# Router logits from the raw sums instead of the normed rows, with the first two experts' ranks computed apart

## The chip, the cores and the metric

The kernel runs on one core of a Trainium2 chip. The metric is the device time of one execution in microseconds (us), measured over several executions. The median of three runs of the kernel before is 3284.68 us (3284.26 to 3285.56).

## The reference, cut to what matters

The program is a stack of layers on 512 tokens of width 1024: two layers of a mixer, a cross attention and a dense feed-forward net (`first_block`), then one layer of attention, retention and a mixture of experts (`second_block`). The change touches what lies between the mixer's output sum and the experts:

```
h = h + mix                                   # the raw sum, x_tok
hn = h * rsqrt(mean(h*h) + 1e-6) * norm_moe_w # rms norm, row factor and column weights
group_logits  = hn @ w_group  + b_group       # 8 columns
expert_logits = hn @ w_expert + b_expert      # 64 columns
...
best group by softmax, its two best experts per token, gates from their softmax
every expert: (silu(hn_e @ w1) * (hn_e @ w3)) @ w2 on the tokens that chose it
h = h + sum of the two experts' rows times their gates
out = rms_norm(h, norm_final_w)
```

Since the row factor is one number per token and the norm weights are one number per column, `hn @ w` equals the row factor times `h @ (norm_moe_w * w)`.

## The kernel before, in words

Everything is fp32. Five engines run programs written out by hand, one method for each stage and engine (`merge_pe`, `router_dve` and so on), joined by counting semaphores; `at(mark)` is the semaphore value at which a step is done. PSUM banks are taken from and given back to one list (`Banks`), so a bank that is taken waits for whoever drained it last. NT = 4 tiles of 128 tokens; KD = 8 blocks of 128 columns.

**Mixer out.** `project_out_pe` multiplies by `w_out` in two halves of 512 columns. For the second half the tiles go in the order (0, 1), (2), (3), each over two weight pieces, twelve matmuls to a tile and piece. After tile 2 it calls `turned(0)`, which transposes the normed rows of tiles 0 and 1; inside tile 3, between its two pieces, it calls `turned(1)`, which does nothing. VectorE adds each half to the raw sum `x_tok` (`add_dve`), and after each tile's second half runs `normed(i)`: `rms_dve` makes the argument of the root, GpSimd takes the power (`root_pool`), VectorE writes the normed row to `hn_low` with its columns regrouped. ScalarE squares and sums the raw row first (`square_act`).

**Router.** `router_pe` transposes the normed rows of tiles 2 and 3 (`rows_to_T_pe_f32`), ScalarE copies them out of PSUM to `xT` (`hn_turned_act`), and 32 matmuls of 72 columns (64 records in the trace, since each fp32 matmul is recorded twice) make the logits. `router_dve` adds the bias and runs a chain of 20 small instructions, each of which waits for the one before, up to `both`, a 0/1 table of each token's two experts. Then `rank` (4 matmuls with a triangle and with ones: how many earlier tokens chose the same expert), `count` (4 matmuls of 64 columns), `local` (VectorE: the rank where the expert was chosen), and for each pair of experts `chosen`, a one-hot table with which TensorE gathers the tokens' rows (`gather_pe`, 16 matmuls for a pair). The gather reads the normed rows split in two, `hn_high` (ScalarE, rounded) and `hn_low` (VectorE, the rest, `hn_split_dve`).

**Experts.** 64 experts, each with three matrices of 2 MB. SyncE loads them in one fixed order into slots; a slot is free when a mark is reached. `experts_pe` declares eight slots: two of 1 MB (`att`, `outs`) used once, and six of 2 MB in this order: `mT` (free when the mixer's last tile is summed), `01`, `20`, `12` (free with the last weight pieces of the mixer), `norms` (free when tile 3's normed row is written, `("moe_norm", "rms", 3)`), `xT` (free when the logits are done). From then on a slot comes free when its expert's matmuls are done. For an expert TensorE runs `upper_pe` (w1 and w3, 16 matmuls, 32 records) and `lower_pe` (w2).

**Loads.** ScalarE's queue issues the router's small tables in `router_act`: `tri`, `router_w` (72 columns by 1024 rows; partition p holds rows 8p to 8p+7, one run of 2304 B for each partition), `router_b`, `down8`, `iota64`.

Of the kernel before, what the change touches and what calls it, by code (L numbers as in the profile page):

```python
# [12 lines left out]
ALU = mybir.AluOpType  # L13
# [51 lines left out]
PC_ALL = PC_GATE + 2 * KD  # L65
# [126 lines left out]
class Net:  # L192
# [2233 lines left out]
    def merge_dve(self, e):  # L2426
# [32 lines left out]
    def router_pe(self, e):  # L2459
        e.begin("router")  # L2460
        banks, at = self.banks, self.at
        W = GROUPS + EXPERTS
        bank = banks.take(e, "router")
        e.wait_ge(*at("router_tables", "iota"))
        for i in range(NT):
            if i % 2 == 0:
                self.rows_to_T_pe_f32(e, 2 + i // 2)
            for b in (0, 4):
                e.wait_ge(*at("hnT", i, b))
            for k in range(KD):  # L2470
                ins = e.matmul(bank[:, i * W:(i + 1) * W], self.xT[:, k, i * P:(i + 1) * P], self.router_w[:, k, :],
                               start=(k == 0), stop=(k == KD - 1))
            ins.then_inc(*(e.tick("pe", "router") if i == NT - 1 else e.tick()))
        banks.give(("router",), "logits")
        bank = banks.take(e, "rank")
        e.wait_ge(*at("both"))
        e.wait_ge(*at("ones"))
        both = self.both.rearrange("p i e -> p (i e)")
# [6 lines left out]
        bank = banks.take(e, "count")  # L2485
# [4 lines left out]
        banks.give(("count",), "counted")  # L2490

    def rows_to_T_pe_f32(self, e, i):
        for b in (0, 4):
            bank = self.banks.take(e, "hnT", i, b)
            e.wait_ge(*self.at("moe_norm", "rms", i))
            self.transposes(e, bank, [self.hn_low[:, i, (b + j) * P:(b + j + 1) * P] for j in range(4)]).then_inc(
                *e.tick("pe", "hnT", i, b))
            self.banks.give(("hnT", i, b), "hnT", i, b)

    def router_act(self, e):  # L2500
# [3 lines left out]
        for name, dst, src in (("tri", self.tri, a["c_tri"]),  # L2504
                               ("w", self.router_w, a["router_w"].rearrange("(p t) n -> p t n", p=P)),
# [4 lines left out]
        for i in range(NT):  # L2510
            self.square_act(e, i, self.hn_high[:, i, :], "moe_norm", ("merge_out", "added", 1, i))
            if i:
                self.hn_turned_act(e, i - 1)
                self.hn_high_act(e, i - 1)
        self.hn_turned_act(e, NT - 1)
        self.hn_high_act(e, NT - 1)

    def hn_high_act(self, e, i):

        self.high_of(e, self.hn_high[:, i, :], self.hn_low[:, i, :]).then_inc(*e.tick("hn_high", i))  # L2520

    def hn_split_dve(self, e, i):

        e.wait_ge(*self.at("pe", "hnT", i, 4))
# [36 lines left out]
    def router_dve(self, e):  # L2561
# [32 lines left out]

        e.wait_ge(*at("pe", "rank"))
        e.scalar_tensor_tensor(out=self.local.rearrange("p i e -> p (i e)"), in0=self.both.rearrange("p i e -> p (i e)"),
                               scalar=FAR, in1=self.bank("rank")[:, 0:NT * EXPERTS], op0=ALU.mult,
                               op1=ALU.subtract).then_inc(*e.tick("local"))

# [80 lines left out]
    def gather_pe(self, e, q):  # L2680

        ch = self.chosen[q % 2]
        for half in range(2):
# [4 lines left out]
            for i in range(NT):  # L2688
# [52 lines left out]
    def experts_pe(self, e):  # L2741
# [16 lines left out]
        self.rows_T_pe(e, 0)  # L2758
        self.upper_pe(e, 0)
# [103 lines left out]
    def experts_dve(self, e):  # L2863
        e.begin("experts")
        for n in range(EXPERTS + 1):
            if n < EXPERTS and n % 2 == 0:
# [3 lines left out]
                for i in range(NT):  # L2870
                    e.tensor_tensor(self.rounded(self.chosen[n // 2 % 2][:, i, :, :]),
                                    self.from_far.unsqueeze(1).broadcast_to([P, 2, CAP]),
                                    self.local[:, i, n:n + 2].unsqueeze(2).broadcast_to([P, 2, CAP]),
                                    ALU.is_equal).then_inc(*(e.tick("chosen", n // 2) if i == NT - 1 else e.tick()))
# [293 lines left out]
def columns(inputs):  # L3168
# [17 lines left out]
    out[:, PC_GATE:PC_GATE + 2 * KD] = tile(np.asarray(inputs["b_branch_gate_2"])[0])  # L3186
    return out
# [37 lines left out]
```

## Time and profile before

| | |
|---|---|
| median of 3 runs | 3284.68 us |
| the profiled execution, its own time | 3284.82 us |
| its span, first to last instruction | 3283.0 us |
| mean granted TensorE clock | 0.976 of full speed |
| PE (TensorE matmul) busy | 3094.9 us, 94% |
| DVE (VectorE) busy | 1389.0 us, 42% |
| ACT (ScalarE) busy | 887.1 us, 27% |
| POOL (GpSimd) busy | 134.4 us, 4% |
| DMA | 627.49 MB, 191 GB/s over the span |
| DMA in the last quarter | 426 to 430 GB/s in each fortieth of the span |

The profile is of one execution. Times in its rows are us from the start of the span; a duration named mean or min/median/max is in ns. "PEld" is the loading of weights, which overlaps matmuls. "SPq" and "ACTq" are the instructions with which SyncE and ScalarE start DMAs. A matmul's end is modelled, so neighbouring matmuls overlap in the rows, and their pace is read from start to start. The share of busy time says little here, since the stages differ: the first 2240 us are held by TensorE, the last 900 by the loads.

### The profile page before, as it was taken

To read this page: it belongs to the slowest core of one execution; us is meant where nothing else is said; L and a number is where in the kernel's file an instruction comes from. 1 tells how busy PE (TensorE), PEld (TensorE's weight loads), DVE (VectorE), ACT (ScalarE), POOL (GpSimd) and SP (SyncE) were. 2 spreads that over 40 slices of the span, in tenths; PEclk is the share of its full clock that TensorE was granted. 3 is DMA by queue.
4 is the path that set the end of the run, shared out by engine and by line. 5 is a ranking of instruction groups with operands and counts; after the bars stand their busy time and mean duration, and the time that the engine had idled before them with its cause. 6 is when DMAs were issued, how large, how long until landed. Compare 5 with 4: busy or idle time off the path is not lost.

```text
span 3283.0 us, 34804 instructions
## 1 busy us (share of the span) xinstructions
PE 3094.9 (94%) x14748; PEld 2159.3 (66%) x14748; DVE 1389.0 (42%) x2291; ACT 887.1 (27%) x1408; POOL 134.4 (4%) x118
## 2 busy tenths in 40 slices
PE   9999999999999999999999899998999889999995
PEld 7678688887677778888888787886434334434332
DVE  5675543335586553334777576434211111111112
ACT  3452322222343322222344432332111111111111
POOL 0000000001000000000211010000000000000001
PEclk9999999999999999999999999999999999999998
DMA  5122122333222222322322430235999999999997
GB/s 178 52 77 97 57 93 97 100 108 118 65 64 86 69 80 87 109 97 96 110 68 68 119 102 33 81 112 229 401 429 429 430 429 429 428 426 429 428 429 304
DMA packets 197794, 627.49 MB, mean 191 GB/s; under 512 B 11712, under 2 KB 129216, under 8 KB 172672
## 3 DMA queue, kind: packets, MB, share of 16 engines
q1 hardware_dynamic: 176288, 581.46, 45.5%
q10 hardware_dynamic: 19152, 35.61, 3.0%
q0 software_dynamic: 2192, 8.13, 0.9%
q8 instruction: 118, 1.93, 0.2%
q14 instruction: 44, 0.36, 0.0%
HBM read 600.26 MB, written 22.81 MB: 190 GB/s over the span
## 4 chain that ended last, share of the span: by engine, by line
PE 75%; DVE 10%; DMA 8%; ACT 3%; issue 2%; POOL 2%; ACTq 0%; SPq 0%; DVEq 0%
PE bank L121 72%; PE bank L124 3%; DMA pieces<-in_moe_w 3%; DVE gate_acc L139 2%; DMA highs<-in_moe_w 2%; DMA piece_high<-in_moe_w 2%; DVE x_tok L139 1%; POOL root L136 1%; DVE piece_rounded L136 1%; DVE stat L154 1%; ACT piece_high_rounded L127 1%; DVE probs L142 1%; DVE aprobs L142 1%; ACT probs L127 1%; DVE qs L136 1%
## 5 line engine op out<-in xcount | busy, mean ns | idle before, releaser
L136 DVE TENSOR_TENSOR piece_rounded<-piece,piece_high_rounded 128x2048 fp32r<-128x2048 f32 (+2 forms) x160 | 346.7, 2171 | 527.6 <-ACT piece_high_rounded L127 527.5
L121 PE MATMUL bank<-xT_rounded,piece_high_rounded 128*128 128x512 f32 (+1 forms) x1424 | 541.4, 380 | 12.1 <-DVE xT_low_rounded L136 7.2
L121 PE MATMUL bank<-xT_low_rounded,piece_high_rounded 128*128 128x512 f32 (+1 forms) x1424 | 538.7, 378 | 0.0
L121 PE MATMUL bank<-xT_rounded,piece_rounded 128*128 128x512 f32 (+1 forms) x1424 | 538.4, 378 | 0.0
L136 DVE TENSOR_TENSOR gate_and_hidden<-gate_and_hidden,bank 64x512 f32<-64x512 f32 x64 | 69.3, 1082 | 801.8 <-ACT gate_and_hidden L127 801.8
L127 ACT ACTIVATE piece_high_rounded<-piece 128x2048 fp32r<-128x2048 f32 (+2 forms) x160 | 288.1, 1804 | 254.6 <-DMA piece<-in_ffn_w_down 91.5
L121 PEld LDWEIGHTS bank<-xT_rounded,piece_high_rounded 128*128 128x128 f32 x1424 | 269.1, 189 | 64.2 <-DVE xT_low_rounded L136 8.2
L121 PEld LDWEIGHTS bank<-xT_rounded,piece_rounded 128*128 128x128 f32 x1424 | 269.1, 189 | 49.4
L121 PEld LDWEIGHTS bank<-xT_low_rounded,piece_high_rounded 128*128 128x128 f32 x1424 | 269.1, 189 | 48.1
L121 PE MATMUL bank<-mT_pair,xeT 128*64 128x512 f32 x352 | 178.8, 667 | 22.8 <-issue 22.8
L121 PE MATMUL bank<-xT,xeT 128*64 128x512 f32 x336 | 172.4, 673 | 23.0 <-issue 22.6
L121 PE MATMUL bank<-memory_norms,xeT 128*64 128x512 f32 x320 | 167.1, 683 | 22.2 <-issue 22.2
L127 ACT ACTIVATE gate_and_hidden<-bank 64x512 f32<-64x512 f32 x64 | 37.8, 591 | 479.0 <-PE bank L121 479.0
L139 DVE SCALAR_TENSOR_TENSOR gate_acc<-hT,cols,gate_acc 128x512 f32<-128x512 f32 x240 | 163.2, 743 | 0.0
L121 PE MATMUL bank<-highs,xeT 128*64 128x512 f32 x352 | 155.6, 595 | 2.0 <-DMA pieces<-in_moe_w 2.0
L121 PE MATMUL bank<-piece_high,xeT 128*64 128x512 f32 x352 | 155.6, 595 | 1.9 <-DMA highs<-in_moe_w 1.9
L121 PE MATMUL bank<-pieces,xeT 128*64 128x512 f32 x320 | 141.5, 595 | 1.4 <-DMA piece_high<-in_moe_w 1.4
L121 PE MATMUL bank<-piece_high_rounded,hidT_rounded 128*128 128x512 f32 x352 | 137.3, 390 | 0.0
L121 PE MATMUL bank<-piece_high_rounded,hidT_low_rounded 128*128 128x512 f32 x352 | 137.1, 389 | 0.0
L121 PE MATMUL bank<-piece_rounded,hidT_rounded 128*128 128x512 f32 x352 | 137.1, 389 | 0.0
L121 PE MATMUL bank<-piece_high_rounded,xT_rounded 128*128 128x512 f32 (+1 forms) x320 | 120.9, 378 | 5.3 <-DVE xT_low_rounded L136 2.7
L136 POOL TENSOR_TENSOR root<-root,power 128x1 f32<-128x1 f32 (+2 forms) x60 | 61.0, 1016 | 1444.5 <-DVE root L133 1444.4
(344 smaller groups left out, 4903.1 us busy)
## 6 DMA issues: line engine op xcount, KB each, us to landing
mT_pair<-in_moe_w SPq DMA_DIRECT2D x32, 2048.0 KB, 16.5
pieces<-in_moe_w SPq DMA_DIRECT2D x32, 2048.0 KB, 16.5
piece_high<-in_moe_w SPq DMA_DIRECT2D x32, 2048.0 KB, 16.4
highs<-in_moe_w SPq DMA_DIRECT2D x32, 2048.0 KB, 16.7
xT<-in_moe_w SPq DMA_DIRECT2D x32, 2048.0 KB, 16.7
memory_norms<-in_moe_w SPq DMA_DIRECT2D x31, 2048.0 KB, 16.7
piece<-in_ffn_w_in SPq DMA_DIRECT2D x40, 1024.0 KB, 5.0
piece<-in_w_in SPq DMA_DIRECT2D x20, 1024.0 KB, 4.8
```

Of the source, the lines that this page charges most:

```text
L121: return self.engine.matmul(*a, **k) if self.engine is not None else Nothing()
L124: return self.engine.transpose(*a, **k) if self.engine is not None else Nothing()
L127: return self.engine.activation(*a, **k) if self.engine is not None else Nothing()
L136: return self.engine.tensor_tensor(*a, **k) if self.engine is not None else Nothing()
L139: return self.engine.scalar_tensor_tensor(*a, **k) if self.engine is not None else Nothing()
L142: return self.engine.tensor_tensor_reduce(*a, **k) if self.engine is not None else Nothing()
L154: return self.engine.bn_stats(*a, **k) if self.engine is not None else Nothing()
```

## The change

Four edits. (1) The transposes read `x_tok`, the raw sum, instead of the normed row; tile 2's transposes and the logits of tiles 0 and 1 stand in `turned(1)`, between the two pieces of tile 3. (2) The column weights go into `router_w` by one VectorE multiplication (its load uses the plain row order now, 1024 runs of 288 B, and the norm weights come with the table `cols`); the row factor goes in where the bias is added, tile by tile. (3) Tile 3's normed row is written after `both`; its square on ScalarE comes after the copies of its transposes. (4) The ranks of experts 0 and 1 are made first from 8, 6, 4 and 2 columns, then the whole rank; the counts come after the first gather and its transposes. The slots `xT` and `norms` change places.

```diff
         def turned(i):
-            if i:
+            if i == 0:
+                for j in (0, 1):
+                    self.rows_to_T_pe_f32(e, j)
                 return
+            self.banks.take(e, "router", 0)
             for j in (0, 1):
-                self.rows_to_T_pe_f32(e, j)
+                self.logits_pe(e, j)
+            self.rows_to_T_pe_f32(e, 2)
...
         def normed(i):
-            self.rms_dve(e, i, self.hn_low[:, i, :], self.gain[:, :], "moe_norm", ("moe_norm", "gain"), KD)
+            if i == 0:
+                e.wait_ge(*at("router_tables", "iota"))
+                e.tensor_tensor(self.router_w, self.router_w,
+                                self.cols[:, PC_NORM:PC_NORM + KD].unsqueeze(2).broadcast_to([P, KD, GROUPS + EXPERTS]),
+                                ALU.mult).then_inc(*e.tick("router_w"))
+            if i < NT - 1:
+                self.rms_dve(e, i, self.hn_low[:, i, :], self.gain[:, :], "moe_norm", ("moe_norm", "gain"), KD)
...
+        bank = banks.take(e, "first_rank")
         e.wait_ge(*at("both"))
         e.wait_ge(*at("ones"))
+        e.matmul(bank[:, 0:2 * NT], self.tri, self.both[:, :, 0:2], start=True, stop=False).then_inc(*e.tick())
+        for n in range(1, NT):
+            ins = e.matmul(bank[:, 2 * n:2 * NT], self.ones, self.both[:, 0:NT - n, 0:2], start=False, stop=(n == NT - 1))
...
     def rows_to_T_pe_f32(self, e, i):
...
-            e.wait_ge(*self.at("moe_norm", "rms", i))
-            self.transposes(e, bank, [self.hn_low[:, i, (b + j) * P:(b + j + 1) * P] for j in range(4)]).then_inc(
+            e.wait_ge(*self.at("merge_out", "added", 1, i))
+            self.transposes(e, bank, [self.x_tok[:, i, (b + j) * P:(b + j + 1) * P] for j in range(4)]).then_inc(
...
-                               ("w", self.router_w, a["router_w"].rearrange("(p t) n -> p t n", p=P)),
+                               ("w", self.router_w, a["router_w"].rearrange("(t p) n -> p t n", p=P)),
...
-        for i in range(1, NT):
+        for i in range(1, NT - 1):
             self.hn_split_dve(e, i)
-        e.wait_ge(*at("pe", "router"))
-        e.tensor_tensor(logits, self.bank("router")[:, 0:NT * W].rearrange("p (i w) -> p i w", i=NT),
-                        self.row(self.router_b, W), ALU.add).then_inc(*e.tick("logits"))
+        for i in range(NT):
+            if i == NT - 1:
+                self.rms_arg_dve(e, i, "moe_norm")
+            e.wait_ge(*at("pe", "router", max(i, 2)))
+            e.wait_ge(*at("root", "moe_norm", i))
+            e.scalar_tensor_tensor(out=logits[:, i, :], in0=self.bank("router", i // 3)[:, i * W:(i + 1) * W],
+                                   scalar=self.root[:, i, 0:1], in1=self.router_b, op0=ALU.mult,
+                                   op1=ALU.add).then_inc(*e.tick("logits", i))
...
-
+        self.rms_row_dve(e, NT - 1, self.hn_low[:, NT - 1, :], self.gain[:, :], "moe_norm", ("moe_norm", "gain"), KD)
+        first = self.local[:, :, 0:2]
+        e.wait_ge(*at("pe", "first_rank"))
...
+        self.chosen_dve(e, 0)
+        self.hn_split_dve(e, NT - 1)
...
+        self.add_slot("xT", self.xT[:, :, :].rearrange("p k s -> p (k s)"), ("pe", "router", NT - 1))
         self.add_slot("norms", memory, ("moe_norm", "rms", NT - 1), ("pe", "m_branch", "retention", KD - 1))
-        self.add_slot("xT", self.xT[:, :, :].rearrange("p k s -> p (k s)"), ("pe", "router"))
...
         self.rows_T_pe(e, 0)
+        self.count_pe(e)
```

The order of the instructions on TensorE from tile 2's transposes to the last logits, before (`hn_low` is the normed row, `mT` the mixer's merged input, `xT` the transposed rows):

```order
L124 MATMUL bank<-ident,hn_low 128x128 [waits merge_vector_done,side_loads]
L124 MATMUL bank<-ident,hn_low 128x128 x7
L121 MATMUL bank<-router_w,xT 128x72 [waits router_scalar_done]
L121 MATMUL bank<-router_w,xT 128x72 x7
...
L124 MATMUL bank<-ident,hn_low 128x128 [waits merge_vector_done]
L124 MATMUL bank<-ident,hn_low 128x128 x7
```

and in the change, from the end of tile 3's first piece over its second to tile 3's transposes:

```order
L122 MATMUL bank<-router_w,xT 128x72 [waits router_scalar_done]
L122 MATMUL bank<-router_w,xT 128x72 x7
L122 MATMUL bank<-router_w,xT 128x72 [waits router_scalar_done]
L122 MATMUL bank<-router_w,xT 128x72 x7
L125 MATMUL bank<-ident,x_tok 128x128 [waits merge_vector_done]
L125 MATMUL bank<-ident,x_tok 128x128 x7
L122 MATMUL bank<-piece_high_rounded,mT_rounded 128x512
...
L125 MATMUL bank<-ident,x_tok 128x128 [waits merge_vector_done]
L125 MATMUL bank<-ident,x_tok 128x128 x7
```

Two tiles' logits and one tile's transposes moved ahead of the last twelve matmuls of the mixer's output; before, all of it came behind them.

On the same engine, from `both` to the first gather, before:

```order
L121 MATMUL bank<-both,tri 128x256 [waits router_gpsimd_done,router_vector_done]
L121 MATMUL bank<-both,ones 128x192
L121 MATMUL bank<-both,ones 128x128
L121 MATMUL bank<-both,ones 128x64 x5
L121 MATMUL bank<-hn_high_rounded,chosen_rounded 128x512 [waits experts_vector_done]
```

and in the change:

```order
L122 MATMUL bank<-both,tri 128x8 [waits router_gpsimd_done,router_vector_done]
L122 MATMUL bank<-both,ones 128x6
L122 MATMUL bank<-both,ones 128x4
L122 MATMUL bank<-both,ones 128x2
L122 MATMUL bank<-both,tri 128x256
L122 MATMUL bank<-both,ones 128x192
L122 MATMUL bank<-both,ones 128x128
L122 MATMUL bank<-both,ones 128x64
L122 MATMUL bank<-hn_high_rounded,chosen_rounded 128x512 [waits router_vector_done]
```

Four small matmuls are new ahead of the rank, and the four of the counts are gone from here; the whole rank still stands ahead of the gather.

On VectorE, from `both` on, the change has this order (before, `local` followed `both` at once):

```order
L137 TENSOR_TENSOR both<-oh_g,t_197 128x256 [waits router_vector_done]
L140 SCALAR_TENSOR_TENSOR hn_low<-x_tok,root,norm_room 128x1024
L140 SCALAR_TENSOR_TENSOR local<-both,bank 128x4x2 [waits router_tensor_done]
L137 TENSOR_TENSOR chosen_rounded<-from_far,local 128x128 [waits router_vector_done]
L137 TENSOR_TENSOR chosen_rounded<-from_far,local 128x128 x3
L137 TENSOR_TENSOR hn_low_rounded<-hn_low,hn_high_rounded 128x1024 [waits router_scalar_done]
L140 SCALAR_TENSOR_TENSOR local<-both,bank 128x256 [waits router_vector_done,router_tensor_done]
```

Tile 3's normed row and its split moved here from ahead of the logits.

## Rows read from the trace of the kernel before

**Rows 1.** Stretches: busy us of PE, PEld, DVE, ACT, POOL; clock, DMA share, GB/s.
```profile
2284.00:2286.00 2.00, 2.00 (x12) 0.77 (x10) 1.93 (x3) 0.00 (x0) 0.00 (x0) 1.00 0.46 197
2286.00:2288.00 2.00, 2.00 (x12) 0.78 (x10) 1.11 (x4) 0.00 (x0) 0.00 (x0) 1.00 0.00 0
...
2330.00:2340.00 10.00, 10.00 (x54) 3.81 (x52) 6.32 (x16) 1.57 (x3) 0.00 (x0) 1.00 0.82 319
...
2350.00:3235.00 885.00, 812.19 (x3697) 347.75 (x3696) 125.31 (x228) 124.26 (x229) 0.00 (x0) 0.95 1.01 429
```

**Rows 2.** Timeline of SyncE's queue, the experts' loads: start, us, line, slot.
```profile
2254.03 0.33 SPq L163 DMA_DIRECT2D mT_pair<-in_moe_w  x1
...
2288.72 0.33 SPq L163 DMA_DIRECT2D mT_pair<-in_moe_w  x1
2295.59 0.33 SPq L163 DMA_DIRECT2D piece_high<-in_moe_w  x1
...
2331.43 0.33 SPq L163 DMA_DIRECT2D highs<-in_moe_w  x1
```

**Rows 3.** The chain that ended last, 2237 to 2331 us: start, us, engine and output.
```profile
2237.71 0.70 DVE x_tok L139
...
2248.52 5.50 PE bank L121 x24
...
2254.04 0.70 DVE x_tok L139
...
2256.76 2.10 DVE hn_low L139
...
2258.90 1.09 PE bank L124 x8
2259.99 3.54 PE bank L121 x32
...
2263.55 0.47 DVE logits L136
...
2268.96 0.43 DVE both L136
...
2269.43 9.96 PE bank L121 x32
...
2319.43 0.90 DVE chosen_rounded L136 x4
...
2320.38 11.01 PE bank L121 x48
```

**Rows 4.** Timeline of TensorE: transposes of tiles 1 and 2; counts; first gather.
```profile
2247.43 1.09 PE L124 MATMUL bank<-ident,hn_low 128*128 128x128 f32 x8 [0.72 <-DVE hn_low L139]
...
2253.84 1.04 PE L124 MATMUL bank<-ident,hn_low 128*128 128x128 f32 x8
...
2272.69 1.06 PE L121 MATMUL bank<-both,ones 128*128 128x64 f32 x4
2273.51 0.77 PE L121 MATMUL bank<-hn_high_rounded,chosen_rounded 128*128 128x512 f32 x1
```

**Rows 5.** Groups by line and shape, 2236 to 2300 us: count | busy us, mean ns.
```profile
L127 ACT ACTIVATE xT<-bank 128x512 f32<-128x512 f32 x8 | 4.3, 593 | 3.7 <-PE bank L124 3.7
...
L139 DVE SCALAR_TENSOR_TENSOR extra<-bank,extra 128x64 f32<-128x64 f32 x6 | 1.3, 224 | 0.2
...
L136 DVE TENSOR_TENSOR e<-ends,iota 128x960 f32<-128x960 f32 x1 | 1.2, 1157 | 0.0
```

**Rows 6.** Stretches, columns as in rows 1, where the clock is low.
```profile
2268.00:2277.00 9.00, 7.57 (x24) 6.69 (x25) 2.53 (x11) 0.00 (x0) 0.00 (x0) 0.50 1.00 428
2277.00:2278.00 1.00, 1.00 (x4) 0.80 (x3) 0.00 (x0) 0.60 (x1) 0.00 (x0) 0.65 1.07 459
```

**Rows 7.** Loads on ScalarE's queue: router_w's issue, and landing of tile kr_w.
```profile
2224.01 0.45 ACTq L163 DMA_DIRECT2D router_w<-in_router_w  x1
...
DMA to landing us min/median/max: 4.7/5.1/5.5
```

More of the change, by code:

```diff
@@ L64 @@
 PC_GATE = DEPTH * PC_LAYER
-PC_ALL = PC_GATE + 2 * KD
+PC_NORM = PC_GATE + 2 * KD
+PC_ALL = PC_NORM + KD
 SLOT = KD * BANK // 2
@@ L2461, in router_pe @@
         banks, at = self.banks, self.at
[L2462 to L2475, printed above, removed]
+        self.rows_to_T_pe_f32(e, NT - 1)
+        self.logits_pe(e, 2)
+        banks.give(("router", 0), "logits", 2)
+        banks.take(e, "router", 1)
+        self.logits_pe(e, NT - 1)
+        banks.give(("router", 1), "logits", NT - 1)
+        bank = banks.take(e, "first_rank")
         e.wait_ge(*at("both"))
         e.wait_ge(*at("ones"))
+        e.matmul(bank[:, 0:2 * NT], self.tri, self.both[:, :, 0:2], start=True, stop=False).then_inc(*e.tick())
+        for n in range(1, NT):
+            ins = e.matmul(bank[:, 2 * n:2 * NT], self.ones, self.both[:, 0:NT - n, 0:2], start=False, stop=(n == NT - 1))
+        ins.then_inc(*e.tick("pe", "first_rank"))
+        banks.give(("first_rank",), "first_local")
+        bank = banks.take(e, "rank")
         both = self.both.rearrange("p i e -> p (i e)")
@@ L2484, in router_pe, with count_pe @@
         banks.give(("rank",), "rank_copied")
-        bank = banks.take(e, "count")
+    def count_pe(self, e):
+        bank = self.banks.take(e, "count")
         for j in range(NT):
@@ L2489, in router_pe, with logits_pe @@
         ins.then_inc(*e.tick("pe", "count"))
-        banks.give(("count",), "counted")
+        self.banks.give(("count",), "counted")
+    def logits_pe(self, e, i):
+        W = GROUPS + EXPERTS
+        bank = self.bank("router", i // 3)
+        e.wait_ge(*self.at("router_w"))
+        for b in (0, 4):
+            e.wait_ge(*self.at("hnT", i, b))
+        for k in range(KD):
+            ins = e.matmul(bank[:, i * W:(i + 1) * W], self.xT[:, k, i * P:(i + 1) * P], self.router_w[:, k, :],
+                           start=(k == 0), stop=(k == KD - 1))
+        ins.then_inc(*e.tick("pe", "router", i))
     def rows_to_T_pe_f32(self, e, i):
@@ L2509, in router_act @@
             e.dma_start(dst, src).then_inc(*e.lands("side_loads", "router_tables", name))
[L2510 to L2514, printed above, removed]
+        square = lambda i: self.square_act(e, i, self.hn_high[:, i, :], "moe_norm", ("merge_out", "added", 1, i))
+        square(0)
+        square(1)
+        self.hn_high_act(e, 0)
+        square(2)
+        self.hn_turned_act(e, 0)
+        self.hn_turned_act(e, 1)
+        self.hn_high_act(e, 1)
+        self.hn_turned_act(e, 2)
+        self.hn_high_act(e, 2)
         self.hn_turned_act(e, NT - 1)
+        square(NT - 1)
         self.hn_high_act(e, NT - 1)
     def hn_high_act(self, e, i):
+        e.wait_ge(*self.at("moe_norm", "rms", i))
         self.high_of(e, self.hn_high[:, i, :], self.hn_low[:, i, :]).then_inc(*e.tick("hn_high", i))
     def hn_split_dve(self, e, i):
-        e.wait_ge(*self.at("pe", "hnT", i, 4))
         e.wait_ge(*self.at("hn_high", i))
@@ L2593, in router_dve @@
                         self.t8.unsqueeze(2).broadcast_to([P, NT, GROUPS, PER_GROUP]), ALU.mult).then_inc(*e.tick("both"))
+        self.rms_row_dve(e, NT - 1, self.hn_low[:, NT - 1, :], self.gain[:, :], "moe_norm", ("moe_norm", "gain"), KD)
+        first = self.local[:, :, 0:2]
+        e.wait_ge(*at("pe", "first_rank"))
+        e.scalar_tensor_tensor(out=first, in0=self.both[:, :, 0:2], scalar=FAR,
+                               in1=self.bank("first_rank")[:, 0:2 * NT].rearrange("p (i e) -> p i e", i=NT),
+                               op0=ALU.mult, op1=ALU.subtract).then_inc(*e.tick("first_local"))
+        e.wait_ge(*e.own())
+        self.chosen_dve(e, 0)
+        self.hn_split_dve(e, NT - 1)
         e.wait_ge(*at("pe", "rank"))
+        e.wait_ge(*at("chosen", 0))
         e.scalar_tensor_tensor(out=self.local.rearrange("p i e -> p (i e)"), in0=self.both.rearrange("p i e -> p (i e)"),
@@ L2598, in router_dve, with chosen_dve @@
                                op1=ALU.subtract).then_inc(*e.tick("local"))
+    def chosen_dve(self, e, n):
+        for i in range(NT):
+            e.tensor_tensor(self.rounded(self.chosen[n // 2 % 2][:, i, :, :]),
+                            self.from_far.unsqueeze(1).broadcast_to([P, 2, CAP]),
+                            self.local[:, i, n:n + 2].unsqueeze(2).broadcast_to([P, 2, CAP]),
+                            ALU.is_equal).then_inc(*(e.tick("chosen", n // 2) if i == NT - 1 else e.tick()))
     def counts_dve(self, e):
@@ L2687, in gather_pe @@
                 e.wait_ge(*self.at("hn_split", i))
-            for i in range(NT):
                 for part, hn in enumerate((self.hn_high, self.hn_low)):
@@ L2865, in experts_dve @@
         for n in range(EXPERTS + 1):
-            if n < EXPERTS and n % 2 == 0:
+            if 0 < n < EXPERTS and n % 2 == 0:
                 e.wait_ge(*self.at("local"))
@@ L2869, in experts_dve @@
                     e.wait_ge(*self.at("pe", "rows", n // 2 - 2, 1))
[L2870 to L2874, printed above, removed]
+                self.chosen_dve(e, n)
             if n >= 1:
@@ L3186, in columns @@
     out[:, PC_GATE:PC_GATE + 2 * KD] = tile(np.asarray(inputs["b_branch_gate_2"])[0])
+    out[:, PC_NORM:PC_NORM + KD] = tile(np.asarray(inputs["norm_moe_w_2"])[0])
     return out
```

## The prediction

> **What bounds the kernel now.** I read the stretches first, then SyncE's queue, then the chain that ended last. From 2350 us on the 16 DMA engines are busy all the time and move 429 GB/s while TensorE has gaps [rows 1]: the end of the kernel is the end of this stream of loads. What happens earlier counts only as far as it moves the stream. Before 2350 us the stream has holes: its engines are idle through 2286 to 2288 us and for half of the two microseconds before [rows 1], and at 0.81 or 0.82 in three stretches of ten microseconds, 2290 to 2300, 2310 to 2320 and 2330 to 2340, of which the last is shown [rows 1]. In each hole SyncE waits for a slot: the second load into `mT` is issued at 2288.72, when expert 0's upper matmuls are done, the next at 2295.59, and the one after the last hole at 2331.43 [rows 2]. From there on the stream never waits. So the end of the kernel moves with the issue at 2331.43, and that hangs on TensorE's chain: `chosen` for experts 4 and 5, then a gather and expert 3's upper matmuls [rows 3], and, further back, expert 0's first matmul. The question is how much earlier the first gather starts and ends.
>
> **Tile 3's norm leaves the path.** Before, tile 3's add starts at 2254.04 and lasts 0.70; its transposes start at 2258.90 [rows 3]. Between lie square, root and the normed row, 2258.90 - 2254.74 = 4.16 us. Now the transposes follow the add at about 0.04, the usual step: 4.12 us less.
>
> **The work put in front of it.** Between tile 2's matmuls and tile 3's sum TensorE now also does two tiles' logits, 3.54 us (the 32 records that follow 2259.99 [rows 3]), and the transposes of tile 2. Those take 1.04 us with their modelled end [rows 4], and the next matmuls start before it; I take 0.88. Together 4.42 us more. A wait goes: the second tile's transposes stood 0.72 us for their normed row and began at 2247.43 [rows 4]; the raw row is there, and with the overlap of two such groups it is 0.9. So tile 3's sum comes 3.5 us later, at about 2257.5 in place of 2254.0. At the start of tile 3's transposes -4.12 + 3.5 = -0.6, and the logits of tiles 2 and 3 behind them cost 3.54 as before: the last logits end near 2262.9 in place of 2263.5.
>
> Do these logits find their inputs? ScalarE's copies take 593 ns each [rows 5], two to a tile. Tiles 0 and 1 are copied behind the square of tile 2, which ends at about 2249.1; their four copies overlap and end at about 2250.1 and 2251.2. Tile 3's first piece ends at about 2250.2 (2247.4 and twelve matmuls, 2.75 us by the 24 of 5.50 [rows 3]). No stall above 0.1 us. Tile 3's square, behind its copies, ends near 2261.2, and the root near 2262.7: before the last logits, by only 0.2 us. This is the narrowest place on the path; if it slips, the gain shrinks by what it slips.
>
> **The bias.** One instruction on 288 columns held 0.50 us (2263.55 to the next at 2264.05, 0.47 of it its own) [rows 3]. Three of the four new ones run ahead of the last logits; the last costs what a small one of this kind does, 224 ns [rows 5], so about 0.25 less. `both` is ready 0.87 earlier.
>
> **router_w's multiplication** has 576 columns. The nearest row, 960 columns, takes 1157 ns [rows 5], so 0.7 us; it lies where VectorE waits for square and root behind tile 0's add. For tile 3 these 2.02 us are 2254.74 to 2256.76 [rows 3], and VectorE does 0.15 us of work in them. Nothing. If that cover were gone, tile 0's norm would be up to 0.7 later, and it has slack too.
>
> **From both to the gather.** TensorE starts on the ranks at 2269.43 and on the gather at 2273.51 [rows 3, 4]: 4.08 us for the rank and the counts. The change takes out the counts' 4 matmuls (8 records) and puts in 4 (8 records) of 8 to 2 columns. The last four count records took 2273.51 - 2272.69 = 0.82 us, 0.2 each [rows 4]. Bounds for the new 8: from nothing to the same 1.6 us, since each loads 128 x 128 weights whatever its columns. I take the upper end, whose row is nearest. Then the gather can start 4.08 after `both` as before. VectorE is ready earlier: normed row 2.10 [rows 3], small local 0.22, `chosen` 0.90 [rows 3] make 3.3 with steps. The whole rank is in front of the gather on TensorE, so the first-two-experts' short cut gives nothing as long as TensorE is the later of the two; with the new records at nothing VectorE would set the start and the gain would be 0.8 more. Tile 3's split is done by about 2273.0, while the gather reaches tile 3 only at its seventh matmul, about 2.6 us in. The counts' new place is TensorE's wait for VectorE's two copies ahead of expert 0: nothing, or 0.1.
>
> On short matmuls the trace and the notes part. In rows, 64-column records take 0.2 us at the low clock [rows 4]. The Trainium skill, page "TensorE: Matmul & The Clock Gate", section "Wait — 56ns, not 53.3ns?", says that the distance of small matmuls does not fall below about 25 ns; by that alone the eight would cost 0.2 us and the sum would be -1.6 in place of -0.9. It counts no weight loads.
>
> **The clock.** TensorE idles while VectorE runs its chain, and the granted clock is 0.50 (1.2 GHz) from before 2268 until between 2277 and 2278 [rows 6]; about nine of the gather's 16 matmuls run in it, at 0.43 us each (512 columns at 1.2 GHz), the rest at 0.23 like the mixer's, 5.50 us for 24 [rows 3]. The idle stretch stays 5.6 us or so, so the clock will fall again. If it comes back as long after TensorE's restart as before, the whole 0.87 is kept. If it comes back at the same time as before, two more matmuls run slow and the gain is 0.46. I take 0.7.
>
> **The stream.** Its start, the `mT` load at 2254.03 [rows 2], waits for tile 3's sum: 3.5 later. Six loads ran from there to about 2284.9, by the share of 0.46 in the two microseconds from 2284 [rows 1]. Now they end near 2288.4, while the next slot comes free at 2288.72 - 0.7 = 2288.0: the first hole closes, and that load starts 0.4 late or in time. The next hole (about 2 us) takes this up, so from 2294 on the slots set the times again. The `norms` slot now waits for tile 3's normed row, near 2270.7; it is the sixth load and needed at 2283, so SyncE's standing there (nothing else is behind it until 2288) costs nothing. The later loads of experts 0 and 1 land 3.5 later, expert 1's w3 at about 2281, used at 2288.
>
> **The sum.** -0.6 (path to the logits) -0.25 (bias) + 0 (multiplication, ranks, counts) + 0.15 (clock, between 0 and 0.4) = -0.7 us. The profiled execution took 3284.82, so 3284.1 by it; that is 0.14 above the median, so 3284.0 as a median.
>
> **The rivals.**
> - *The late start goes through.* If the holes behind 2288 did not take up the stream's delay, the end would be up to 3.5 us later: 3288.2. It decides when the six loads end later than the slot is freed and the next two waits of SyncE have no idle DMA behind them. Against it: three more stretches with about 2 us idle each [rows 1]. 0.07, with a lower clock for longer at the gather (+1).
> - *router_w comes late.* Its load is issued at 2224.01 [rows 7] and needed behind tile 0's add, at 2238.4 [rows 3], 14.4 us later. The nearest load with short runs (1024 of 128 B, `kr_w`) lands in 4.7 to 5.5 us [rows 7]. Were it later than 14.4, VectorE would stand at the multiplication with the adds, norms and TensorE's transposes behind it; slower by over 0.2% of the whole, 6.6 us, from a landing of 21 us on: 3291.3. 0.02. The Trainium skill, "DMA: Bandwidth & Descriptors", section "Specifications", speaks for this one: runs under 512 B do not reach line rate.
> - *The clock is back sooner, or the short ranks are nearly free.* Then the gather ends 1.7 to 2.5 us earlier: 3282.3 to 3283.1. 0.13.
> - *The whole norm of tile 3 is gained* (4.1 us, 3280.6), if the late sum of tile 3 cost nothing. The order on TensorE speaks against it. 0.03.
>
> **How the numbers follow.** The forecast has 0.75. A measurement of this kernel can tell about 0.2%, 6.6 us, from no change. Even all holes of the stream together, about 9 us of idle, less the late start of 3.5, give less than 6.6, so faster by over 0.2% has 0.02; slower has 0.02, from the late load; within is 0.96. The range takes in the runs' own spread (1.3 us), the third case and half of the first: 3282.2 to 3286.2.
>
> **What would show it.** Right: SyncE's first `mT` load near 2257.5, the last 72-column records near 2262.9, `both` near 2268.1, the gather from 2272.6, expert 0 from about 2280.9, the issue that was at 2331.43 near 2330.7, no idle DMA between 2286 and 2288. Wrong: small-rank records much shorter than 0.2 us, a root of tile 3 that ends behind the last logits, or a stream that is saturated from 2288 on.

## The result, and the profile after

| | before | change |
|---|---|---|
| median of 14 runs each | 3285.44 us (3282.35 to 3289.54) | 3291.68 us (3288.86 to 3295.45) |
| ratio, 95% interval | | 1.0017 [1.001, 1.0024] |
| profiled execution, its span | 3284.82, 3283.0 us | 3290.51, 3288.6 us |

I forecast 3284.0 (3282.2 to 3286.2), 0.7 us below the median. The change is about 6 us slower. That is within 0.2% by its ratio, but far outside the range.

SyncE's queue shows where the time arises, first in the change:

```profile
2218.38 0.51 SPq L164 DMA_DIRECT2D att_single<-in_moe_w  x1
...
2257.06 0.33 SPq L164 DMA_DIRECT2D mT_pair<-in_moe_w  x1
...
2270.19 0.33 SPq L164 DMA_DIRECT2D memory_norms<-in_moe_w  x1
2286.09 0.33 SPq L164 DMA_DIRECT2D mT_pair<-in_moe_w  x1
2292.95 0.33 SPq L164 DMA_DIRECT2D piece_high<-in_moe_w  x1
...
2330.37 0.33 SPq L164 DMA_DIRECT2D highs<-in_moe_w  x1
...
3236.82 0.33 SPq L164 DMA_DIRECT2D memory_norms<-in_moe_w  x1
```

and, beside [rows 2], the load that comes before the router, and the last one of all, before:

```profile
2219.07 0.51 SPq L163 DMA_DIRECT2D att_single<-in_moe_w  x1
...
3231.98 0.33 SPq L163 DMA_DIRECT2D xT<-in_moe_w  x1
```

Take three stretches. Up to the load `att_single` the change is 0.69 us earlier, which I take as chance: the builds of before below whose first part is not slowed have this load between 2217.69 and 2221.07. At the issue that [rows 2] has at 2331.43 it is 1.06 earlier. From this issue to the last load it takes 3236.82 - 2330.37 = 906.45 us; before, 3231.98 - 2331.43 = 900.55. So the stretch of which I had said that it would run as before takes **5.9 us more**. The rest behind the last issue (51.8 and 51.0) makes up the spans: -1.06 + 5.90 + 0.8 = 5.6.

The last issue is not quite the end of the stream. The last packet of the loads ends at 3246.80 in the change and at 3243.23 before, by the trace's packet records. Counted up to there, the stretch grew from 911.80 to 916.43 us, that is by 4.6; the other 1.3 us of the 5.9 come from the last load being issued closer to its own end (9.97 us ahead of it, where before has 11.25). What follows the last packet took 41.8 us in the change and 39.8 before, but it varies between 39.1 and 41.2 among the kernels below whose stream has the rate of before and whose first 2220 us are as before, so a difference there is in part chance.

The stretches of [rows 1], in the change:

```profile
2284.00:2286.00 2.00, 2.00 (x12) 0.84 (x10) 0.50 (x3) 0.00 (x0) 0.00 (x0) 1.00 0.98 418
2286.00:2288.00 2.00, 2.00 (x12) 0.72 (x9) 1.25 (x2) 0.59 (x1) 0.00 (x0) 1.00 0.99 418
2330.00:2340.00 10.00, 10.00 (x52) 3.87 (x52) 6.31 (x16) 1.57 (x3) 0.00 (x0) 1.00 0.86 341
2350.00:3235.00 885.00, 816.66 (x3671) 345.65 (x3672) 124.15 (x227) 123.60 (x228) 0.00 (x0) 0.94 1.01 426
```

The first hole, 2284 to 2288, is closed, as forecast (share 0.98 and 0.99). In the last row the engines are as busy as before (1.01) but move 426 GB/s, not 429: the same share of time, less data. The DMA view of 2500 to 3000 us says the same for the experts' queue, q1, before:

```profile
DMA packets 19397, 214.23 MB, mean 428 GB/s; under 512 B 2624, under 2 KB 2624, under 8 KB 6848
...
q1 hardware_dynamic: 14096, 205.27, 96.1%
```

and in the change:

```profile
DMA packets 19270, 213.39 MB, mean 427 GB/s; under 512 B 2599, under 2 KB 2599, under 8 KB 6765
...
q1 hardware_dynamic: 14047, 204.54, 96.1%
```

Both have 96.1% of 16 engines' time; 205.27 MB became 204.54. So the queue did not wait more; its packets take longer. The trace's own packet records, which no view lists, show it. The figures here and below are for the expert loads' 16 KB packets from 2350 us to the end of the loads. Before, 98.7% of them took 611 ns at most; in the change 53% took longer, mostly 614 and 621 ns. Leaving out the few over 640 ns, the mean rose from 611.04 to 613.31. Summed and divided by 16 engines, these durations make 3.2 us of the 4.6, and the packets over 640 ns another 0.8; the remaining 0.6 or so I cannot assign.

### The profile page after: what moved, and what is told of

Same layout as the page of the kernel before. It is cut to its first block, busy times and chain, and to the rows that moved or that the text cites. A ratio compares the mean times of both kernels' runs of the same rounds, so it can differ in the third digit from the quotient of the medians.

```text
span 3288.6 us, 34824 instructions
## 1 busy us (share of the span) xinstructions
PE 3103.8 (94%) x14756; PEld 2156.3 (66%) x14756; DVE 1389.7 (42%) x2296; ACT 887.2 (27%) x1408; POOL 134.7 (4%) x118
## 4 chain that ended last, share of the span: by engine, by line
PE 80%; DVE 11%; issue 3%; ACT 2%; DMA 2%; POOL 2%; ACTq 0%; SPq 0%; DVEq 0%; POOLq 0%
PE bank L122 77%; PE bank L125 3%; DVE gate_acc L140 3%; DVE x_tok L140 1%; POOL root L137 1%; DVE piece_rounded L137 1%; DVE stat L155 1%; DVE probs L143 1%; ACT piece_high_rounded L128 1%; DVE aprobs L143 1%; DMA pieces<-in_moe_w 1%; DMA highs<-in_moe_w 1%; ACT probs L128 1%; DVE qs L137 1%; DVE xT_low_rounded L137 0%
## 5 line engine op out<-in xcount | busy, mean ns | idle before, releaser
L122 PE MATMUL bank<-mT_pair,xeT 128*64 128x512 f32 x352 | 187.0, 693 | 21.8 <-issue 21.8
L122 PE MATMUL bank<-memory_norms,xeT 128*64 128x512 f32 x336 | 180.6, 700 | 23.4 <-issue 23.0
```

Source lines behind the costliest of these rows:

```text
L122: return self.engine.matmul(*a, **k) if self.engine is not None else Nothing()
```

## Why a packet should take longer

The loads, their sizes and their source were not changed. Three other things were, without an edit that looks like it. **Theory A, the place in SBUF.** `cols` grew from 314 to 322 columns, 1256 to 1288 B, and rounded to 32 B every tile allocated behind it moved by 32 B: the statistics, the weight slots (52224 B = 51 x 1024 before, 52256 now; they hold the slots `01`, `20` and `12`), the work room (101376 and 101408; it holds `mT`) and `xT`. Only the slot `norms` lies ahead of `cols`, at 32896 B, and moves in none of these kernels. **Theory B, the width of `cols` in HBM**, which may move what lies behind it there. **Theory C, the slots' order**: `xT` and `norms` changed places. Each of the three can be done alone. The expectations also name a **theory D**, the prediction's own rival that the late start of the stream goes through; against it speaks already that the issue near 2331 came 1.06 us earlier, so the late start had been taken up by then.

**before_plus32**, theory A alone in the kernel before:

```diff
         self.cols = self.sb("cols", [P, PC_ALL])
+        self.sb("spare", [P, 8])
```

> Edit: the kernel before with a spare tile of 8 columns (32 B in each partition) behind the table cols, so that every expert slot but norms lies 32 B further, as in the change. No work changes. Theory A (the 32 B shift of the slots in SBUF makes the experts' 16 KB packets longer): in the profile the packets' share above 611 ns rises from 2% to about half, the stage from 2350 us runs at 427 GB/s instead of 429, and the time is 5 to 7 us above the kernel before. Theory B (the longer table cols shifts the inputs' addresses in HBM): no difference from the kernel before. Theory C (the order of the slots xT and norms): no difference. Theory D (the late start of the stream goes through): no difference.

Measured: 3292.5 us (3286.59 to 3295.49) beside a shared 3287.04, ratio 1.0011 [1.0002, 1.002], with 53% of the packets above 611 ns. Its queue and its stretch:

```profile
2333.34 0.33 SPq L163 DMA_DIRECT2D highs<-in_moe_w  x1
...
3239.61 0.33 SPq L163 DMA_DIRECT2D xT<-in_moe_w  x1
```

```profile
2350.00:3235.00 885.00, 814.71 (x3672) 346.04 (x3672) 124.23 (x227) 124.67 (x230) 0.00 (x0) 0.94 1.01 427
```

3239.61 - 2333.34 = 906.27 us, where before has 900.55 (to the last packet 916.4, as in the change). An unused tile of 32 B gives the whole loss of the stream. So it is the place of the tiles behind `cols` that costs the time; which of them matters is another question, and comes below.

**before_hbm**, theory B alone: the array is 8 columns wider, the tile is not.

```diff
-                               ... ("cols", self.cols[:, :], a["cols"]),
+                               ... ("cols", self.cols[:, :], a["cols"][:, 0:PC_ALL]),
...
-    out = np.zeros((P, PC_ALL), np.float32)
+    out = np.zeros((P, PC_ALL + 8), np.float32)
```

> Edit: the kernel before with the input table cols 8 columns wider in HBM, of which only the first 314 are loaded, so that SBUF is as before and only what lies in HBM behind cols can move. Theory A (SBUF shift): no difference from the kernel before, packets at 611 ns. Theory B (HBM addresses): 5 to 7 us slower, half of the packets above 611 ns. Theories C and D: no difference.

Measured: 3285.95 (3282.64 to 3289.21), 0.9999 [0.999, 1.0008]; 1.5% of packets above 611 ns, 429 GB/s, 2331.76 to 3232.49 = 900.73 us. Theory B falls.

**after_slots**, the change with the slots' order of before:

```diff
-        self.add_slot("xT", ...)
         self.add_slot("norms", memory, ...)
+        self.add_slot("xT", ...)
```

> Edit: the change with the slots norms and xT in the order of the kernel before. Theory A (SBUF shift), B (HBM addresses), D (late start): as slow as the change, about 3291 us, 0.17% above the kernel before. Theory C (order of the slots): back to the kernel before or 1 us below it.

Measured: 3290.53 (3284.84 to 3293.07), 1.0009 [1.0, 1.0018]; 53% above 611 ns, 426 GB/s, 906.42 us. Theory C falls.

**after_plus32**, the change with a spare tile of 8 columns behind `cols`, so 64 B off:

> Edit: the change with a spare tile of 8 more columns behind cols, so that the slots lie 64 B instead of 32 B beyond where they were in the kernel before. Theory A (32 B shift of the slots in SBUF, and 64 B is a good place again): packets back at 611 ns, 429 GB/s, and the time 0.5 to 2.5 us below the kernel before, since the issue that was at 2331.43 us comes about 1 us earlier. Theory B (HBM addresses), C (slot order) and D (late start of the stream): as slow as the change, about 3291 us.

Measured: 3289.73 (3288.22 to 3292.53), 1.0008 [0.9998, 1.0017]; 48% above 611 ns, 427 GB/s, 904.26 us. The expectation that 64 B would be a good place was wrong; it is only a little better than 32 B.

## The change without the shift

**after_far** keeps `cols` at 314 columns and puts the norm weights into a tile of their own behind `xT`, where nothing follows (with one small load more):

```diff
-PC_ALL = PC_NORM + KD
+PC_ALL = PC_GATE + 2 * KD
...
         self.xT = self.sb_twin("xT", [P, KD, S])
+        self.norm_cols = self.sb("norm_cols", [P, KD])
```

> Edit: the change with the norm weights in a small tile of their own behind xT (one small load more), cols as long as before, so that every tile lies where it lay in the kernel before. Theory A (the moved SBUF tiles make the experts' packets longer): packets back at 611 ns for all but 2%, 429 GB/s, the time 0 to 3 us below the kernel before, and 5 to 7 below the change. Theory E (the change's order of work or its issue times in SyncE's queue make the packets longer, and the 32 B tile did so by chance of another kind): as slow as the change, half of the packets above 611.

Measured: 3285.95 (3282.8 to 3288.82) beside a shared 3287.42, ratio 0.9997 [0.9988, 1.0006]; 1.4% above 611 ns.

```profile
2222.43 0.51 SPq L164 DMA_DIRECT2D att_single<-in_moe_w  x1
...
2334.15 0.33 SPq L164 DMA_DIRECT2D highs<-in_moe_w  x1
...
3234.87 0.33 SPq L164 DMA_DIRECT2D memory_norms<-in_moe_w  x1
```

```profile
2350.00:3235.00 885.00, 808.82 (x3694) 347.63 (x3696) 124.20 (x227) 124.93 (x232) 0.00 (x0) 0.96 1.01 428
```

3234.87 - 2334.15 = 900.72 us: the stream has its length back, with the change's own order of work, its order of slots and the wider array in HBM still in place. What the change does on the engines is worth nothing that can be measured in the whole time.

**before_plus1024** (the same spare tile as in before_plus32, with 256 columns):

> Edit: the kernel before with a spare tile of 1024 B in each partition behind cols, so that all later tiles move but keep their place within 1024 B. Theory A1 (where the tiles lie against some power of two up to 1024 B decides): packets at 611 ns, no difference from the kernel before. Theory A2 (any other addresses, as the distance to the tiles ahead of cols): half of the packets above 611 and 4 to 6 us slower.

Measured: 3287.71 (3282.17 to 3288.86), 0.9999 [0.999, 1.0008]; 1.0% above 611 ns, 900.54 us. A move as such costs nothing.

## Which distance counts, and a surprise

Two kernels moved parts against each other. **before_work32** leaves the slots and moves the work room and `xT` by 32 B; **before_slots32** moves the slots by 32 B and puts 992 B behind them, so that the work room and `xT` move by 1024 B. The edit of before_work32:

```diff
         self.high_slots = [...]
+        self.sb("spare", [P, 8])
         self.work_at = (nc.sbuf_base + 31) // 32 * 32
```

> Edit: the kernel before with 32 B between the high slots and the work room: slots 01, 20 and 12 stay, mT, xT and all tiles of the work room (one-hot tables, hidden rows, outputs) move by 32 B. If the place of the written slot decides for its own packets: loads into mT and xT are long, those into 01, 20, 12 and norms stay at 611 ns, a third of the effect, 1.5 to 2 us. If the tiles that the engines read and write at the same time decide: all of it or nothing, alike for all slots.

> Edit: the kernel before with 32 B ahead of the weight slots and 992 B behind them: slots 01, 20 and 12 move by 32 B, the work room, mT and xT by 1024 B. If the place of the written slot decides: loads into 01, 20 and 12 are long, the others at 611 ns, half of the effect, 2 to 3 us. If the tiles of the work room decide: nothing.

Measured: 3322.53 (3320.82 to 3328.89), 1.0113 [1.0098, 1.0128], and 3328.84 (3324.94 to 3333.57), 1.0124 [1.0109, 1.014]. For the stream neither expectation came out. From the issue that follows the last hole to the last issue, before_work32 takes 901.04 us, with 5% of packets above 611 ns, and before_slots32 904.01 us, with 17%; together that is far less than the 53% of both blocks moved by 32 B. Nor are the long packets those into the moved slots alone. The packet records do not name their load, so I count them off in order of start, 128 to a load, which is off by some packets at each border. In before_work32 the moved `mT` and `xT` have 7% and 4%, the others 3 to 6%. In before_slots32 the moved `01`, `20` and `12` have 17 to 31%, but `norms`, which did not move, has 15%. And in before_plus32 and the change, `norms` has 38% beside 51 to 60% in the five slots that moved, where before it had 2%. **So a packet's length is not decided by the place of its own target alone**: packets into a slot that stayed get longer when the tiles beside it move. Which of the tiles does it, and how, stays open.

Nearly all of the 35 and 41 us lies elsewhere, though: `att_single` is issued at 2252.20 and 2259.42, in place of 2219.07. The loss is in the dense part. Groups by line of 0 to 2220 us, before:

```profile
L121 PE MATMUL bank<-xT_low_rounded,piece_high_rounded 128*128 128x512 f32 (+1 forms) x1424 | 538.7, 378 | 0.0
...
L121 PE MATMUL bank<-piece_high_rounded,hidT_rounded 128*128 128x512 f32 x352 | 137.3, 390 | 0.0
```

and in before_work32:

```profile
L121 PE MATMUL bank<-xT_low_rounded,piece_high_rounded 128*128 128x512 f32 (+1 forms) x1411 | 539.7, 383 | 0.0
...
L121 PE MATMUL bank<-piece_high_rounded,hidT_rounded 128*128 128x512 f32 x352 | 139.5, 396 | 0.0
```

The mean of one rose from 378 to 383 ns and from 390 to 396. The means with "+1 forms" mix shapes, but by shape it is the same: the 128x512 records of the first kind went from 390 to 395 ns. The granted clock is 0.99 over this part in both. These matmuls take one operand from a weight slot and the other from the work room or from `xT`. Over the 4272, 1056 and 960 records of the three largest kinds in this part (three groups each, of 1424, 352 and 320) the rise makes some 27 of the 33 us (4.3, 6.2 and 2.5 ns each). The two groups of 256 matmuls of `memT` with a weight slot, neither of which moved, are together no slower (126.1 us before, 125.6 here). In before_plus32, where both moved together, `att_single` is issued at 2221.06, so at most 2.0 us of its time lie there.

Three kernels, each run once, ask for the unit. One run says little about the time, but the length of the stream in a trace is steady: it is 900.5 to 901.0 us in every kernel with short packets.

> The kernel before with a spare tile of 32 columns (128 B) behind cols: weight slots, work room and xT lie 128 B further, as one block. Theory A1 (16 KB packets land at full rate only where the slots lie at a multiple of 1024 B or some large power of two): about half of the expert loads' packets take longer than 611 ns, the stretch 2350 to 3235 shows 427 GB/s or less, and from the load issue near 2331 to the last one pass 905 to 907 us instead of 900.6. Theory A2 (a multiple of 128 B is enough, since 32 and 64 B were bad and 1024 B was not): 429 GB/s, 2% of the packets or fewer above 611 ns, 900 to 901 us. In neither does the dense part before the router change: the attention load stays at 2218 to 2220.

> The kernel before with a spare tile of 128 columns (512 B) behind cols. Theory A1 with 1024 B as the unit: as at 32 B, 427 GB/s and 905 to 907 us from the issue near 2331 to the last. With 512 B as the unit, or with theory A2: 429 GB/s and 900 to 901 us. The dense part does not change in either.

> The kernel before with 512 B of spare room between the weight slots and the work room, so the slots stay where they were and the work room and xT lie 512 B further. With 32 B there, the dense part took 33 us more: its matmul records rose from 380 to 384 ns and from 390 to 396 ns on average. Theory D1 (what counts is how far the matmul's two operands lie apart within 512 B or less): as before, the attention load at 2218 to 2222 and those means at 380 and 390 ns. Theory D2 (any distance other than a multiple of 1024 B costs): the attention load at 2240 to 2260 and means of 383 to 385 and 395 to 397 ns. The expert loads keep 429 GB/s in both.

Measured for before_plus128: 3286.79 us; 34% above 611 ns, 427 GB/s, 3233.80 - 2330.06 = 903.74 us. 128 B is not enough. before_plus512: 3284.91; 1.2%, 429 GB/s, 900.49 us. before_work512: 3285.64; 1.4%, 428 GB/s, 900.72 us, `att_single` at 2219.97, and its groups are those of before again:

```profile
L121 PE MATMUL bank<-xT_low_rounded,piece_high_rounded 128*128 128x512 f32 (+1 forms) x1424 | 538.1, 378 | 0.0
...
L121 PE MATMUL bank<-piece_high_rounded,hidT_rounded 128*128 128x512 f32 x352 | 137.2, 390 | 0.0
```

**before_plus256** halves the distance once more:

> The kernel before with a spare tile of 64 columns (256 B) behind cols. If the unit is 512 B: some of the 16 KB packets above 611 ns (fewer than the 34% at 128 B, say 5 to 30%), 427 to 428 GB/s, and 901.5 to 903.5 us from the load issue near 2332 to the last. If the unit is 256 B: under 2% above 611 ns, 429 GB/s, 900 to 901 us.

Measured, in one run: 3287.14 us (before on the same chip 3287.2), 1.4% above 611 ns, 428 GB/s.

```profile
2333.43 0.33 SPq L163 DMA_DIRECT2D highs<-in_moe_w  x1
...
3234.01 0.33 SPq L163 DMA_DIRECT2D xT<-in_moe_w  x1
```

900.58 us: a shift of 256 B costs the loads nothing. Set side by side, from the issue near 2331 to the last issue (and to the last packet): shifted by 32 B 906.3 (916.4), 64 B 904.3 (915.6), 128 B 903.7 (914.8), 256 B 900.6 (911.9), 512 B 900.5 (911.8), 1024 B 900.5 (911.8), not shifted 900.6 (911.8). The 64 B are those of after_plus32, the rest are the kernel before. Shifts of 96, 160 or 224 B were not tried, so that multiples of 256 B are the rule is a guess from three of them.

**after_plus480** is the change with 120 spare columns, so at 512 B:

> The change with 120 spare columns (480 B) behind cols, so that together with the 32 B of the change itself everything behind cols lies 512 B further than in the kernel before, as one block. Theory A1 with a unit of 512 B or less (512 B further cost nothing in the kernel before, 128 B cost 3.2 us from the load issue near 2332 to the last one, 32 B cost 5.7): 428 or 429 GB/s from 2350 to 3235, under 2% of the packets above 611 ns, 900 to 901 us from the issue near 2330 to the last one, and a time of 3284 to 3287 us, a ratio of 0.999 to 1.0005. A rival, that something in the change's own order slows the stream and the far tile had hidden that by chance: 427 GB/s, 905 us, and a ratio of 1.001 to 1.002.

Measured: 3285.98 (3283.57 to 3289.41) beside 3287.2, ratio 0.9995 [0.9986, 1.0005]; 1.7% above 611 ns, 428 GB/s, 3234.27 - 2333.27 = 901.0 us. A second way to the same result as after_far: at 512 B the change costs nothing, and gains nothing that can be measured. No version here is measurably faster than the kernel before.

## Why the prediction was wrong, step by step

The chain from tile 3's sum to the second group of experts in the change, beside [rows 3]:

```profile
2257.07 0.70 DVE x_tok L140
...
2257.82 1.09 PE bank L125 x8
2258.91 3.54 PE bank L122 x32
...
2262.47 0.30 DVE logits L140
...
2267.70 0.43 DVE both L137
...
2268.18 8.59 PE bank L122 x32
...
2278.97 13.95 PE bank L122 x64
...
2316.81 0.90 DVE chosen_rounded L137 x4
...
2317.75 12.57 PE bank L122 x48
```

- **Tile 3's norm off the path, work put in front of it: right.** First load into `mT` at 2257.06 (forecast 2257.5), transposes 0.05 behind the add, last logits at 2262.45 (2262.9). Both are 0.4 us early, less than the 0.7 us that the execution had gained already; so this part is sized right to 0.3 us.
- **The narrowest place held.** Tile 3's square comes before its root, and GpSimd's root of tile 3 starts at 2261.52 and takes 0.54, so it ends at 2262.06, 0.4 before the last logits.
- **Bias: 0.18 gained, forecast 0.25** (from the bias to `both` 2267.70 - 2262.47 = 5.23; before, 5.41). **router_w's multiplication is hidden.** Groups by shape of 2236 to 2300 us:

```profile
L140 DVE SCALAR_TENSOR_TENSOR logits<-bank,root,router_b 128x72 f32<-128x72 f32 x4 | 1.0, 288 | 1.6 <-PE bank L122 1.6
...
L137 DVE TENSOR_TENSOR router_w<-router_w,cols 128x576 f32<-128x576 f32 x1 | 0.8, 752 | 0.0
```

`both` starts at 2267.70 (2268.1). The multiplication takes 0.75 us, as estimated (0.7), and no step of the chain waits for it.
- **Both to gather, forecast 4.08: 4.07**, in TensorE's timeline:

```profile
2268.18 0.60 PE L122 MATMUL bank<-both,tri 128*128 128x8 f32 x2 [5.74 <-DVE both L137]
2268.63 1.42 PE L122 MATMUL bank<-both,ones 128*128 128x6 f32 x6
2269.91 1.20 PE L122 MATMUL bank<-both,tri 128*128 128x256 f32 x2
2270.90 1.59 PE L122 MATMUL bank<-both,ones 128*128 128x192 f32 x6
2272.25 0.77 PE L122 MATMUL bank<-hn_high_rounded,chosen_rounded 128*128 128x512 f32 x1
```

The eight new records hold 2268.18 to 2269.91, 1.73 us, 0.22 each; I had taken 1.6. The prediction set beside this a sum of -1.6 in place of -0.9; its own sum is -0.7, and -0.9 is that sum without the 0.15 for the clock. By the 25 ns floor of the Trainium skill ("TensorE: Matmul & The Clock Gate", section "Wait — 56ns, not 53.3ns?") they would be 0.2 us in all at the least. The row decides, for fp32 records that load 128 x 128 weights each at the low clock.
- **The clock: off by more than the whole gain, twice.** Stretches in the change (the column before the last two is the granted clock):

```profile
2270.00:2272.00 2.00, 2.00 (x8) 1.82 (x8) 1.86 (x7) 1.06 (x1) 0.00 (x0) 0.50 0.96 410
2272.00:2274.00 2.00, 2.00 (x8) 1.72 (x8) 0.93 (x2) 0.00 (x0) 0.00 (x0) 0.64 0.96 410
2274.00:2276.00 2.00, 2.00 (x10) 1.61 (x9) 0.00 (x0) 0.60 (x1) 0.00 (x0) 1.00 1.07 459
2318.00:2324.00 6.00, 6.00 (x20) 4.23 (x22) 0.00 (x0) 1.20 (x2) 0.00 (x0) 0.73 1.02 424
```

and before:

```profile
2274.00:2276.00 2.00, 2.00 (x6) 1.53 (x5) 0.00 (x0) 0.00 (x0) 0.00 (x0) 0.50 1.03 442
2320.00:2326.00 6.00, 5.62 (x24) 3.56 (x26) 0.32 (x2) 1.19 (x2) 0.00 (x0) 1.00 1.01 427
```

At 2274 the clock is back at 1.00 (2.4 GHz) in the change and still 0.50 (1.2 GHz) before; [rows 6] has it back only after 2277. The gather group lasts 8.59, not 9.96, and expert 0's upper matmuls start 2.63 us earlier (1.94 beyond the early start; forecast 0.7). That is my third rival, from the clock and not from free ranks. But then the clock falls behind VectorE's chain for experts 4 and 5 (0.73 in 2318 to 2324, where before has 1.00), and the group of 48 takes 12.57, not 11.01 [rows 3]. It gives back 1.56. In both kernels TensorE had stood idle for 3.17 us just before this group; why the clock fell after it in one and not in the other is not shown. The same holds in all four other builds of the change (12.48 to 12.57). Counted from `att_single`, the issue near 2331 is 0.37 us earlier in the change and 0.35 to 0.64 in those four. Forecast 0.7: the sum was right in sign and near in size, with two large terms in it that I had not seen.
- **The stream takes up its late start: right.** The `norms` slot's load is issued at 2270.19 (2270.7) and delays nothing; no idle DMA from 2284 to 2288, the next slots on time. The rival that the late start goes through did not occur. `router_w` came in time as well: it landed 6.0 us after its issue (before, 5.4), and the chain has no step that waits for it.
- **"From there on the stream never waits. So the end of the kernel moves with the issue at 2331.43": this step failed.** Its first sentence is right. The second took for granted that a saturated stream of unchanged loads has a fixed length. It was 5.9 us longer to the last issue, 4.6 to the last packet, and the runs show the reason: the 32 B that `cols` grew. With them more than half of the 16 KB packets took over 611 ns, mostly 614 and 621; without them (after_far) or with 480 B more (after_plus480) the change has the stream of before. The allocation was in the diff's reach (a table with eight more columns, tiles placed one behind the other), but I costed it as a load of no weight and had no rival for the place of what lies behind it. My sign "wrong: a stream that is saturated from 2288 on" looked for waits and would not have shown it; the one that would is 429 GB/s in [rows 1], becoming 426.

## What to carry to other kernels

When an edit makes a tile in SBUF larger, list the offsets of every tile behind it, above all the targets of the loads that bound the kernel and the operands of its matmuls, and keep them where they are, or move them all together; in this kernel shifts of 256, 512 and 1024 B cost nothing, those of 32, 64 and 128 B did. When a saturated stream of unchanged loads changes its length, compare GB/s at equal DMA share and the duration of one packet before looking for waits. A gain at one stall can be given back by the clock a few microseconds later: read the granted clock over the whole stretch up to the point that counts.

## What the runs showed that I had not expected

- The length of the 16 KB packets of the loads depends on where tiles lie in SBUF: 611.04 ns in the mean with the tiles behind `cols` at the place of before and 256, 512 and 1024 B from it (611.03 to 611.05), 613.3 ns at 32 B, 612.8 at 64 B, 612.4 at 128 B. It is 0.4% of the rate and 3 to 6 us here. It is not simply the target's own place: `norms` begins 128 B beyond a multiple of 1024 in every kernel, its packets are as short as the others in the kernel before, and they get longer when the other tiles move. Nor does each load suffer: at 32 B, counted off in order of start, 70 to 77% of the packets of w3 and w2 are above 611 ns, but only 9 to 11% of w1's. Why w1's are spared, and what in the chip has this grain, was not tried and stays open.
- Matmuls ran 1 to 2% slower (378 to 383 ns, 390 to 396) when the two regions that hold their operands were moved against each other by 32 B. They did not when the two were moved by 512 B against each other (one run), nor when both were moved by 32 B together. It cost 33 us in a dense part of 2220 us. Distances between 32 and 512 B were not tried; nor was a third region told apart from these, since `xT` and the work room moved as one.
- In the change TensorE starts on the ranks 1.25 us earlier (2268.18, before 2269.43), and the clock is back at 2.4 GHz 5.3 us after that start instead of 8.3; at a later place, after an idle stretch of the same length as before, it falls where before it did not. Both recur in five builds, with net -0.4 us; what moves the clock's changes was not tried.
